# Prompt attention with its output products one unit late, opened by 20 unused products

## What is computed

```python
s_c = einsum(q, kc) * scale + bias ; p_c = masked_softmax(s_c) ; o_c = p_c @ vc      # compressed keys, 32
s_s = einsum(q, k_sel) * scale + bias ; p_s = masked_softmax(s_s) ; o_s = p_s @ v_sel # selected blocks
s_w = einsum(q, kw) * scale + bias ; p_w = masked_softmax(s_w) ; o_w = p_w @ vw       # sliding window
o = g[..., 0:1] * o_c + g[..., 1:2] * o_s + g[..., 2:3] * o_w
```

## Time and profile before

| what | value |
|---|---|
| median of 3 runs | 1857.3 us (1855.72 to 1863.38) |
| the profiled execution, its own time | 1855.83 us |
| its span, first to last instruction | 1854.0 us |
| mean granted clock of TensorE | 0.962 |
| PE busy | 1757.1 us, 95% |
| DVE busy | 816.4 us, 44% |
| ACT busy | 528.7 us, 29% |
| POOL busy | 703.4 us, 38% |

### The profile page before, as it was taken

The page is one execution under the profiler, slowest core; times in us unless marked ns, Lnnn a source line. Parts: engine busy times, 40 slices in busy tenths (PEclk is TensorE's granted clock), DMA queues, the critical chain, the costliest instruction groups (busy, mean ns, idle before and its releaser), DMA issues.

```text
span 1854.0 us, 35860 instructions
## 1 busy us (share of the span) xinstructions
PE 1757.1 (95%) x15660; PEld 1672.2 (90%) x15660; DVE 816.4 (44%) x1645; ACT 528.7 (29%) x908; POOL 703.4 (38%) x282
## 2 busy tenths in 40 slices
PE   6989888889979998999999999999999999999998
PEld 5977777579857996999999999999999999999998
DVE  4261686323473444554530445443245555014531
ACT  5232555323331222332211222322223222112221
POOL 1200000013214011656644555656565655446642
PEclk8988799999979997999999999999999999999999
DMA  5540520522101000222222221332222222222222
GB/s 146 122 63 23 167 81 13 159 84 74 47 10 48 4 4 27 87 74 77 77 85 81 91 88 49 103 103 70 92 78 82 72 89 74 86 92 81 71 72 92
DMA packets 159419, 140.83 MB, mean 76 GB/s; under 512 B 16186, under 2 KB 154974, under 8 KB 158878
## 3 DMA queue, kind: packets, MB, share of 16 engines
q1 hardware_dynamic: 159262, 138.53, 25.3%
HBM read 132.62 MB, written 10.02 MB: 77 GB/s over the span
## 4 chain that ended last, share of the span: by engine, by line
PE 69%; DVE 1%; POOL 0%; ACT 0%; issue 0%
PE ps L310 60%; PE ps L2163 8%; PE ps L2626 0%; PE ps L2352 0%; PE ps L2605 0%; PE ps L2611 0%; PE ps L494 0%; PE ps L2423 0%; PE ps L543 0%; DVE y_gated L2876 0%; DVE mixf L2878 0%; DVE mix_lo L2872 0%; PE ps L491 0%; POOL mix_lo L2668 0%; PE ps L492 0%
## 5 line engine op out<-in xcount | busy, mean ns | idle before, releaser
L271 POOL TENSOR_TENSOR w_lo<-w_raw,w_hi 128x2048 fp32r<-128x2048 f32 (+3 forms) x109 | 459.3, 4214 | 781.4 <-ACT w_hi L265 781.2
L310 PE MATMUL ps<-h_hi,w_hi 128*128 128x288 f32 x1792 | 385.0, 296 | 0.0
L310 PE MATMUL ps<-h_hi,w_lo 128*128 128x288 f32 x1792 | 384.4, 295 | 0.0
L310 PE MATMUL ps<-h_lo,w_hi 128*128 128x288 f32 x1792 | 384.3, 295 | 0.0
L265 ACT ACTIVATE w_hi<-w_raw 128x2048 fp32r<-128x2048 f32 (+3 forms) x109 | 190.0, 1743 | 482.9 <-PE ps L310 442.1
L310 PEld LDWEIGHTS ps<-h_hi,w_hi 128*128 128x128 f32 x1792 | 287.2, 188 | 0.3
L310 PEld LDWEIGHTS ps<-h_hi,w_lo 128*128 128x128 f32 x1792 | 286.9, 188 | 0.0
L310 PEld LDWEIGHTS ps<-h_lo,w_hi 128*128 128x128 f32 x1792 | 286.9, 188 | 0.0
L310 PE MATMUL ps<-g_hi,w_hi 128*128 128x288 f32 x704 | 151.6, 296 | 0.0
L310 PE MATMUL ps<-g_hi,w_lo 128*128 128x288 f32 x704 | 151.0, 295 | 0.0
L310 PE MATMUL ps<-g_lo,w_hi 128*128 128x288 f32 x704 | 151.0, 295 | 0.0
(11 more groups left out here) (502 smaller groups left out, 3002.0 us busy)
## 6 DMA issues: line engine op xcount, KB each, us to landing
w_raw<-in_ffn_up SPq DMA_DIRECT2D x44, 1024.0 KB, 5.1
w_raw<-in_ffn_down SPq DMA_DIRECT2D x16, 768.0 KB, 4.6
w_raw<-in_w_in_odd SPq DMA_DIRECT2D x12, 1024.0 KB, 5.2
w_raw<-in_ffn_down SPq DMA_DIRECT2D x16, 640.0 KB, 4.3
w_raw<-in_w_in_even SPq DMA_DIRECT2D x7, 1024.0 KB, 5.3
w_raw<-in_w_in_even SPq DMA_DIRECT2D x6, 872.0 KB, 10.1
BT<-rv SPq DMA_DIRECT2D x8, 520.0 KB, 3.9
seg<-in_cache_cmp_kv SPq DMA_DIRECT2D x32, 128.0 KB
```

The lines of the kernel that those rows point to most:

```text
L271: pool.tensor_tensor(slab_view(wlo[slot], st), slab_view(raw[slot], st), slab_view(whi[slot], st).bitcast(F32), ALU.subtract).then_inc(w_l ...
L310: last = pe.matmul(ps[:, bank + 2 * j + half, 0:HT], w[slot][:, c:c + 128], x[:, xs + t, half * HT:(half + 1) * HT], start=(t == 0 and n = ...
```

## The change

Three things are edited. First, at the end of the compression PE gets 20 products of 512 columns, whose result in bank 3 nobody reads. Second, PTs, PTw and PTc get a second buffer each, and `den` four places, so that the transposed weights of one unit stay while those of the next are made. Third, the order of the streams: PE does the outputs of u-1 between the transposes of u and `scores(u+2)`, and DVE does the weighting of u-1 ahead of `masked_max(u+2)`. The waits follow: a copy waits for the outputs of two units before, the exponentials for the weighting of four units before. The core of the diff:

```diff
+            def keep_warm(pe, bank, width, count):
+                for _ in range(count):
+                    pe.matmul(ps[:, bank, 0:width], hhi[:, 0, 0:128], hhi[:, 1, 0:width], start=True, stop=True)
...
                     outputs(1)
+                    keep_warm(pe, 3, 512, 20)
...
-            PTs = r.take("PTs", [128, 4, 128])
-            PTw = r.take("PTw", [128, 4, 128])
-            PTc = r.take("PTc", [32, 128])
+            PTs = [r.take("PTs", [128, 4, 128]), at("PTs", [128, 4, 128], F32, RAW0)]
+            PTw = [r.take("PTw", [128, 4, 128]), at("PTw", [128, 4, 128], F32, RAW0 + 2048)]
+            PTc = [r.take("PTc", [32, 128]), at("PTc", [32, 128], F32, RAW0 + 4096)]
             mx = r.take("mx", [128, 2, 3])
-            den = r.take("den", [128, 2, 3])
+            den = r.take("den", [128, 4, 3])
...
                         if u + 2 <= U:
                             pe.wait_ge(s_taken, u + 2)
                         pe.transpose(ps[0:32, 4, 256:384], sC[s][:, :], ident[:, :]).then_inc(pt_ready, 1)
+                        if u >= 1:
+                            outputs(u - 1)
                         if u + 2 < U:
                             scores(u + 2)
-                        pe.wait_ge(pt_act, u + 1)
-                        pe.wait_ge(pt_dve, u + 1)
...
-                        last.then_inc(o_ready, 1)
+                    outputs(U - 1)
...
                         dve.wait_ge(pt_ready, u + 1)
+                        if u >= 2:
+                            dve.wait_ge(o_ready, u - 1)
+                        dve.tensor_copy(PTw[s][:, 0:qt + 1, :], ps[:, 6, 0:128 * (qt + 1)].rearrange("p (a b) -> p a b", b=128)).then_inc(pt_dve, 1)
...
                         if u >= 1:
...
+                            weighted(u - 1)
                         if u + 2 < U:
                             masked_max(u + 2)
-                        dve.wait_ge(o_ready, u + 1)
...
+                    weighted(U - 1)
...
-                        if u >= 2:
-                            act.wait_ge(o_taken, u - 1)
+                        if u >= 4:
+                            act.wait_ge(o_taken, u - 3)
```

More of the change, by code:

```diff
@@ L1627, in scores, with outputs @@
                         last.then_inc(s_ready, 1)
+                    def outputs(u):
+                        h, qt, s = u // 4, u % 4, u % 2
+                        g = h // 4
+                        pe.wait_ge(pt_act, u + 1)
+                        pe.wait_ge(pt_dve, u + 1)
+                        if u >= 1:
+                            pe.wait_ge(o_taken, u)
+                        O = ps[:, 7, 0:192]
+                        pe.matmul(O[:, 0:64], PTc[s][:, :], vc[0:32, 2, 64 * g:64 * g + 64], start=True, stop=True)
+                        for n, (PT, c0) in enumerate(((PTs[s], 896), (PTw[s], 1152))):
+                            for kt in range(qt + 1):
+                                last = pe.matmul(O[:, 64 * (n + 1):64 * (n + 2)], PT[:, kt, :], zq[:, kt, c0 + 64 * g:c0 + 64 * g + 64],
+                                                 start=(kt == 0), stop=(kt == qt))
+                        last.then_inc(o_ready, 1)
                     scores(0)
@@ L1631, in _ @@
                         h, qt, s = u // 4, u % 4, u % 2
-                        g = h // 4
                         pe.wait_ge(p_ready, u + 1)
@@ L1680, in masked_max, with weighted @@
                         dve.tensor_scalar(mx[:, s, :], mx[:, s, :], -1.0, None, ALU.mult).then_inc(m_ready, 1)
+                    def weighted(u):
+                        h, qt, s = u // 4, u % 4, u % 2
+                        dve.wait_ge(o_ready, u + 1)
+                        O, out = ps[:, 7, 0:192], onat[:, qt, 64 * h:64 * h + 64]
+                        dve_chain(dve, dve.tensor_scalar(out, O[:, 0:64], den[:, u % 4, 0:1], None, ALU.mult))
+                        dve_chain(dve, dve.scalar_tensor_tensor(out, O[:, 64:128], den[:, u % 4, 1:2], out, ALU.mult, ALU.add))
+                        dve.scalar_tensor_tensor(out, O[:, 128:192], den[:, u % 4, 2:3], out, ALU.mult, ALU.add).then_inc(o_taken, 1)
                     masked_max(0)
@@ L1687, in _ @@
                         dve.wait_ge(pt_ready, u + 1)
-                        if u >= 1:
[L1689 to L1695, removed]
+                        if u >= 2:
+                            dve.wait_ge(o_ready, u - 1)
+                        dve.tensor_copy(PTw[s][:, 0:qt + 1, :], ps[:, 6, 0:128 * (qt + 1)].rearrange("p (a b) -> p a b", b=128)).then_inc(pt_dve, 1)
+                        dve.wait_ge(p_ready, u + 1)
+                        dve_chain(dve, dve.tensor_scalar(den[:, u % 4, :], den[:, u % 4, :], 1e-30, None, ALU.max))
+                        dve_chain(dve, dve.reciprocal(den[:, u % 4, :], den[:, u % 4, :]))
+                        dve_chain(dve, dve.tensor_tensor(den[:, u % 4, :], den[:, u % 4, :], gpr[:, qt, 3 * h:3 * h + 3], ALU.mult))
+                        if u >= 1:
+                            weighted(u - 1)
                         if u + 2 < U:
                             masked_max(u + 2)
-                        dve.wait_ge(o_ready, u + 1)
[L1699 to L1702, removed]
+                    weighted(U - 1)
                 @block.scalar
@@ L1709, in exps @@
                         act.wait_ge(m_ready, u + 1)
-                        if u >= 2:
-                            act.wait_ge(o_taken, u - 1)
-                        act.activation(sC[s][:, :], sC[s][:, :], ACT.Exp, bias=mx[:, s, 0:1], accum_out=den[:, s, 0:1])
-                        act.activation(sS[s][:, 0:nk], sS[s][:, 0:nk], ACT.Exp, bias=mx[:, s, 1:2], accum_out=den[:, s, 1:2])
-                        act.activation(sW[s][:, 0:nk], sW[s][:, 0:nk], ACT.Exp, bias=mx[:, s, 2:3], accum_out=den[:, s, 2:3]).then_inc(p_ready, 1)
+                        if u >= 4:
+                            act.wait_ge(o_taken, u - 3)
+                        d = u % 4
+                        act.activation(sC[s][:, :], sC[s][:, :], ACT.Exp, bias=mx[:, s, 0:1], accum_out=den[:, d, 0:1])
+                        act.activation(sS[s][:, 0:nk], sS[s][:, 0:nk], ACT.Exp, bias=mx[:, s, 1:2], accum_out=den[:, d, 1:2])
+                        act.activation(sW[s][:, 0:nk], sW[s][:, 0:nk], ACT.Exp, bias=mx[:, s, 2:3], accum_out=den[:, d, 2:3]).then_inc(p_ready, 1)
                     exps(0)
                     for u in range(U):
-                        qt = u % 4
+                        qt, s = u % 4, u % 2
                         act.wait_ge(pt_ready, u + 1)
[L1719 to L1722, removed]
+                        if u >= 2:
+                            act.wait_ge(o_ready, u - 1)
+                        act.copy(PTc[s][:, :], ps[0:32, 4, 256:384]).then_inc(ptc_act, 1)
+                        act.copy(PTs[s][:, 0:qt + 1, :], ps[:, 5, 0:128 * (qt + 1)].rearrange("p (a b) -> p a b", b=128)).then_inc(pt_act, 1)
                         if u + 1 < U:
```

## The result

| what | before | after |
|---|---|---|
| median of 4 runs | 1856.9 us | 1907.0 us (1897.86 to 1914.62) |
| ratio to before, 95% interval | | 1.0261 [1.0233, 1.0288] |
| the profiled execution, own time | 1855.83 us | 1903.18 us |
| its span | 1854.0 us | 1901.4 us |
| mean granted clock | 0.962 | 0.939 |

The account below looks back on a forecast made before the run. PE and DVE were both taken as nearly full in the stage. Order +17 us less opening 6.1 gave +11 at the high clock; with low stretches +50, so 1855.8 + 50 + 1.5 = 1907 us, range 1865 to 1938.

Parts of the forecast that it names:

- The order at the high clock: Attention stage: four added DVE waits make a head 16.0 us instead of 13.84, +17 us over eight heads.
- a part of the 1.0: Per head: outputs of two tiles, scores of four tiles and one late exponentials set, together 1.0 us of waits.
- +11 us, were the clock to stay high: Whole stage at 2.4 GHz: +17 us for the order less 6.1 us for the opening, from -2 to +15.
- The clock: Changed stage: falls within the first two heads and later, low 0.6 of the time; with order and opening, +50 us.
- its two heads: A stage head takes 24 us at the low clock and 16.0 us at the high; mean head 20.8 us.
- the one low stretch of the trace: Opening of the stage before, from behind 192.20 to 216.10: about 24 us, taken as the length of low stretches.
- PE's busy share: Changed heads: PE 77% busy against 89% before, nearer the 72% row after which the clock fell, so falls were expected.
- Less the 6.1 us of the opening: First four units: 20 products at the compression's end hold the clock and give back 6.1 us of cold opening.
- The idle gaps: Skill page's rule would keep the changed stage at 2.4 GHz; the forecast went with the trace, which fell despite short gaps.
- The high clock: Rival: the clock stays high through the changed stage, 1868 us; chance 0.16.
- Always low: Rival: the clock falls early and stays low to the end, +75 us, 1932 us; chance 0.12.
- The faster case: Rival: PE's and DVE's waits vanish, DVE's own 11.84 us set the head, 1835 us; chance 0.04.

Follow-up runs that it names:

- the run without the 20 products: The changed kernel without the 20 unused products at the end of the compression; order and buffers as changed: 1908.8 us, ratio 1.028.
- fillers: The changed kernel with 3 more unused products of 512 columns ahead of the transposes of every unit but the first: 1866.9 us, ratio 1.0043.
- the products alone: The kernel before with only the 20 unused products at the end of the compression: 1856.5 us, ratio 0.9986.
- one filler a unit: The kernel before with the 20 products and 1 unused product ahead of the transposes of every unit but the first: 1852.6 us, ratio 0.9965.
- scores first: The changed kernel with scores of u+2 ahead of outputs of u-1 on PE, masked_max ahead of the weighting on DVE: 1852.9 us, ratio 0.9974.
- scores first without the 20 products: The changed kernel with scores ahead of outputs and masked_max ahead of the weighting, 20 products at the compression's end removed: 1856.1 us, ratio 0.9987.
- one filler in the changed order: The changed kernel with 1 unused product of 512 columns ahead of the transposes of every unit but the first: 1886.6 us, ratio 1.0175.

## Why the prediction was right

The forecast of 1907 us was met. Its two large terms are of the right kind and nearly of the right size, one term fell, and that the sum came out to the microsecond is luck.

- **The order at the high clock: right.** Forecast 15.9 to 16.0 us a head, measured 16.28 in two kernels. The single waits of a head, from the run without the 20 products: DVE for the last transpose 1.1 us (forecast 1.2); for output products of four tiles 1.49 (1.4), of three 0.74 (0.5), of two 0.42 (a part of the 1.0). Together that is 3.7 of 4.1; the 0.7 us by which the head is longer than 11.84 + 3.7 is no wait that the profile names. As forecast, PE's waits for copies vanish and PE stands ahead of the last transpose.
- **"+11 us, were the clock to stay high": met by other terms.** With the clock held by fillers the medians show +8 (4.5 to 11.5). But the +11 is 17 for the order less 6.1 for an opening that the products did not give back. Measured are 8 x 2.44 = 19.5 for the order less 4.6 for the opening, which was shorter with the fillers (15.34 us for the first four units instead of 19.91), and the stage of that profile is 14.6 us longer than before (135.5 against 120.9). What made up for the rest lies outside the stage, in that profile 7.2 us, and has no cause shown.
- **The clock: right in kind, in sum by luck.** Forecast: low for 0.6 of the time, in stretches of 24 us, +39 us on top of the order. Measured: 1907.0 - 1866.9 = 40 us; low for 101 of the 145 us from the first last transpose to the 29th, 0.69, in stretches of 7 to 20 us with high ones of 3 to 14 between them. The mean head over those was 20.7 us, forecast 20.8. But the forecast weighted its two heads with shares of time as if they were shares of heads; 0.6 done rightly is 1 / (0.6 / 24 + 0.4 / 16) = 20.0, which would have made the sum +43 and the forecast 1900; 0.69 with 16.28 gives 20.9. The 24 us were read off "the one low stretch of the trace", though the rows have another of 6.6 us. And the sign by which the fall was forecast, PE's busy share, is not borne out by the runs (last section).
- **"Less the 6.1 us of the opening": wrong.** The step that failed took the pause ahead of the stage for the cause of the cold opening. With the products the pause shrank to 1.55 us, and the clock fell 1.0 and 1.4 us into the first scores in the two profiles; the first four units took 19.97 and 19.05 us instead of 19.91. By the ratio the products alone give back 2.6 us, with an interval from 6.1 given back to 0.7 lost, and taking them out of the changed kernel makes 1908.8 of 1907.0; it is the profiles that show the opening no shorter. Whether a stage that PE enters without any pause would stay at 1.00 was not run. What shortened the opening is work inside it: 2.9 us of its first four units came back with one filler a unit, in one profile of each. That the products cost nothing was right. The error did not show in the sum because the stage grew by 53.8 us where the forecast has 49.6, and the rest of the program took less time.
- **The idle gaps.** No wait of PE behind the first scores of the changed stage was longer than 1.4 us, and the clock fell nine times; filling those short waits removed all falls but the first and one 1.5 us ahead of the end. The Trainium skill, page "TensorE: Matmul & The Clock Gate", section "Why this matters for your kernels", puts a drop in the middle of a kernel down to idle gaps between bursts, longer than any wait of PE in this stage. The trace does not agree: by that rule the clock would have stayed at 1.00 behind the opening, and it fell eight more times.
- **The rivals.** The high clock (1868) is what the filled order showed, 1866.9, though with other terms, as said above. Always low (1932) was not seen. The faster case (1835, heads of 11.84 us) was not seen either, but a part of its mechanism exists: with scores first neither engine stands for long and a head takes 13.08 us.

Shown by runs: the two prices, and that PE's and DVE's order must agree. Argued only: the way over PE as the reason of each single wait, and why the clock falls where it does.

## What to carry to other kernels

When work is put off by one unit, read off which engine's chain carries the next unit's release (here scores, `masked_max`, last transpose, copies) and let the postponed work stand behind it on every engine of the chain; done on one engine alone it was worse than on neither (1902 and 1895 us against 1867, with the same fillers). Price a new wait twice: by its length, here 2.44 us a head or 19.5 us in all, and by the clock that PE may lose through it, here 40 us. A run with unused products in the waits separates the two, and may itself be worth keeping.

## What had not been expected of the hardware

Which stretch falls can't be read off PE's busy share. In scores first without the 20 products the clock fell behind 16.80 us with PE busy 15.69 (93%) and behind 23.80 us with 22.51 (95%), while before 98.90 us with PE busy 87.31 (88%) passed at 1.00, and with one filler in the changed order 30.30 us with 25.90 (85%). What tells these apart stays open.

Low stretches need not last: 20 to 24 us in the opening of before and of the products alone, but under 7 us in the changed order with three fillers and with scores first. How long one lasts is open too: in all low stretches shown here but one (scores first without the products, 6.47 of 10.00 us, in part ahead of the stage) PE was busy for 87% of the time or more.
